# Three fast feed-forwards in two parts instead of five, with the seven-product pairs of a part in a row

## The reference

```python
D_FF = 2816
def _swiglu(x, w_in, w_out):
    a, b = jnp.split(x @ w_in, 2, axis=-1)
    return (jax.nn.silu(a) * b) @ w_out
...
    for l in range(DEPTH_2):
        mod = (jax.nn.silu(c) @ ada_w[l] + ada_b[l]).reshape(B, 3, 3, 1, D)
        n = _modulate(_rmsnorm_2(h, norm_g[l, 0]), mod[:, 0, 0], mod[:, 0, 1])
        h = h + 0.5 * mod[:, 0, 2] * _swiglu(n, ffn_w_in[l, 0], ffn_w_out[l, 0])
        ...
        n = _modulate(_rmsnorm_2(h, norm_g[l, 2]), mod[:, 2, 0], mod[:, 2, 1])
        h = h + 0.5 * mod[:, 2, 2] * _swiglu(n, ffn_w_in[l, 1], ffn_w_out[l, 1])
```

## Time and profile before

| what | value |
|---|---|
| median of 3 runs | 3290.63 us (3289.96 to 3294.26) |
| profiled execution, its own time | 3291.03 us |
| its span | 3289.2 us |
| PE busy | 3242.2 us (99%) |
| DVE busy | 2057.6 us (63%) |
| ACT busy | 1461.0 us (44%) |
| DMA | 435.21 MB, mean 132 GB/s |

### The profile page before, as it was taken

The page is one execution under the profiler, slowest core; times in us unless marked ns, Lnnn a source line. Parts: engine busy times, 40 slices in busy tenths (PEclk is TensorE's granted clock), DMA queues, the critical chain, the costliest instruction groups (busy, mean ns, idle before and its releaser), DMA issues.

```text
span 3289.2 us, 52037 instructions
## 1 busy us (share of the span) xinstructions
PE 3242.2 (99%) x22014; PEld 2741.7 (83%) x22014; DVE 2057.6 (63%) x3459; ACT 1461.0 (44%) x2496; POOL 213.5 (6%) x319
## 2 busy tenths in 40 slices
PE   8999999999999999999999999999999999999998
PEld 6878767888888888888778899989998877789997
DVE  6675764678666665665654665666565666466655
ACT  5233565335344422234553444454444455344443
POOL 1000000101000010100000011101010000001110
PEclk9999999999999999999999999999999999999999
DMA  4010102655544365643112366736675321227764
GB/s 152 27 61 31 39 27 96 219 193 185 184 147 147 110 242 192 240 158 108 57 46 88 99 190 174 199 110 174 188 176 158 113 81 47 82 84 178 192 177 120
DMA packets 121193, 435.21 MB, mean 132 GB/s; under 512 B 13936, under 2 KB 16048, under 8 KB 120320
## 3 DMA queue, kind: packets, MB, share of 16 engines
q1 hardware_dynamic: 80928, 286.30, 24.8%
q0 software_dynamic: 40032, 145.58, 17.7%
HBM read 401.41 MB, written 2.10 MB: 123 GB/s over the span
## 4 chain that ended last, share of the span: by engine, by line
PE 91%; DVE 5%; ACT 2%; DMA 1%; issue 0%; POOL 0%; DVEq 0%; ACTq 0%; POOLq 0%
PE ps_run L479 90%; PE ps_run L871 1%; DVE wl L2246 1%; ACT nrm L1369 1%; ACT wh L1369 1%; DMA st<-wst 0%; DVE nrm L2246 0%; DVE X L2253 0%; PE ps_run L1219 0%; DVE HL L2253 0%; DVE nrm L2253 0%; DVE msk L2250 0%; DMA st<-st 0%; ACT HH L1369 0%; ACT bias L1369 0%
## 5 line engine op out<-in xcount | busy, mean ns | idle before, releaser
L2246 DVE TENSOR_TENSOR wl<-st,wh 128x1024 fp32r<-128x1024 f32 (+1 forms) x592 | 721.2, 1219 | 596.2 <-ACT wh L1369 594.3
L479 PE MATMUL ps_run<-HH,wh 128*128 128x512 f32 (+1 forms) x2560 | 911.2, 356 | 11.3 <-DVE HL L2253 3.2
L479 PE MATMUL ps_run<-HH,wl 128*128 128x512 f32 (+1 forms) x2560 | 893.4, 349 | 0.0
L479 PE MATMUL ps_run<-HL,wh 128*128 128x512 f32 (+1 forms) x2560 | 891.3, 349 | 0.0
L1369 ACT ACTIVATE wh<-st 128x1024 fp32r<-128x1024 f32 (+1 forms) x592 | 619.8, 1049 | 586.6 <-PE ps_run L479 453.0
L479 PEld LDWEIGHTS ps_run<-HH,wh 128*128 128x128 f32 x2560 | 485.0, 189 | 82.9 <-DVE HL L2253 6.0
L479 PEld LDWEIGHTS ps_run<-HL,wh 128*128 128x128 f32 x2560 | 485.2, 190 | 63.2 <-issue 3.8
L479 PEld LDWEIGHTS ps_run<-HH,wl 128*128 128x128 f32 x2560 | 484.8, 189 | 63.0
L479 PE MATMUL ps_run<-AH,wh 128*128 128x512 f32 (+1 forms) x1152 | 444.5, 386 | 1.2 <-DVE AL L2246 1.2
L479 PE MATMUL ps_run<-AL,wh 128*128 128x512 f32 (+1 forms) x1152 | 438.3, 381 | 0.0
L479 PE MATMUL ps_run<-AH,wl 128*128 128x512 f32 (+1 forms) x1152 | 438.1, 380 | 0.0
(11 more groups left out here) (453 smaller groups left out, 4026.6 us busy)
## 6 DMA issues: line engine op xcount, KB each, us to landing
st<-wst SPq DMA_DIRECT2D x538, 512.0 KB, 3.4
mb<-ada POOLq DMA_DIRECT2D x144, 512.0 KB, 4.8
st<-wst POOLq DMA_DIRECT2D x54, 512.0 KB, 7.4
st<-st POOLq DMA_DIRECT2D x54, 512.0 KB, 4.6
cw<-cw POOLq DMA_DIRECT2D x4, 1024.0 KB, 6.3
X<-xT SPq DMA_DIRECT2D x8, 256.0 KB, 6.3
X<-xT POOLq DMA_DIRECT2D x8, 256.0 KB, 4.2
out<-X SPq DMA_DIRECT2D x16, 128.0 KB, 1.8
```

The source lines that it names most:

```text
L479: i = self.e.matmul(out, lhsT, rhs, start=start, stop=stop, skip_group_check=True)
L2246: self.e.tensor_tensor(out, a, b, op).then_inc(*self.w.done(*points))
```

## The change

The five parts become two, of the pairs 0 to 5 and 6 to 10, and the down products of a part stand behind its last pair, all eight outputs with 12 or 10 blocks each. Between two seven-product pairs of a part nothing is left. Since a pair's `tail` is now done during the next pair, DVE waits for its own last operation (`w.own()`) before it overwrites a tile that the pair before still reads. `PART_SLOTS` gives the first part 12 slots of `AH`/`AL` and the second 10, and ACT waits before it overwrites a slot of the first part until PE has finished that part's down products. The number of matmuls, of slabs and of adding transfers stays the same; DVE adds 16 down products to `X` in one feed-forward in place of 40.

```diff
-PARTS = ((0, 2), (2, 4), (4, 6), (6, 8), (8, 11))
-PART_SLOTS = ((0, 1, 2, 3), (4, 5, 6, 7), (0, 1, 2, 3), (4, 5, 6, 7), (0, 1, 2, 3, 8, 9))
+PARTS = ((0, 6), (6, 11))
+PART_SLOTS = (tuple(range(12)), tuple(range(10)))
...
-                if k == 4 and i == 7:
+                if k == 1 and i == 7:
                     self.last_linear((key, "down", k, i), specs, hi, lo, ready, outputs, after)
                 else:
-                    finish(self.linear((key, "down", k, i), specs, hi, lo, ready, outputs if k == 4 else beside))
+                    finish(self.linear((key, "down", k, i), specs, hi, lo, ready, outputs))
...
-                if k and p < a + 2:
-                    outputs_of(k - 1, range(4 * (p - a), 4 * (p - a) + 4))
             if k:
-                self.w.stamp("pe part", key, k - 1)
-        self.w.stamp("inputs free", after)
-        outputs_of(4, range(8))
+                self.w.stamp("inputs free", after)
+            outputs_of(k, range(8))
+            self.w.stamp("pe part", key, k)
         self.pad()
...
-        if k >= 2:
-            w.wait_ge("pe part", key, k - 2)
+        if k:
+            w.wait_ge("pe part", key, 0)
         self.half((key, "f", g), m.c1[0], m.AH[slots[0]])
...
-                if k and p < a + 2:
-                    for i in range(4):
-                        finish(self.spend(2 * (PARTS[k - 1][1] - PARTS[k - 1][0])))
-                        if i == 0:
-                            self.finish_pair()
-        self.finish_pair()
-        self.down(after, 4, 6)
+            self.finish_pair()
+            self.down(after, k, 2 * (b - a))
...
                 if step == 1:
+                    w.own()
                     summed(m.c1[x][:, part(0)], 0, x, name, "B", 1)
```

More of the change, by code:

```diff
@@ L2987, in fast_swiglu @@
                     self.plain_pair(key, p, slots, forms)
[L2988 to L2996, removed]
+            self.finish_pair()
+            self.down(key, after, k, into, iter(()), 2 * (b - a))
     def plain_pair(self, key, p, slots, forms):
```

## The result

The changed kernel takes 3421.32 us (median of 4 runs, 3420.60 to 3424.69) against 3291.08 for the kernel before beside it: a ratio of 1.0396 [1.0378, 1.0414], 130 us slower. The profiled execution has a span of 3419.6 us.

A forecast was written before the change was run, and what follows sets the result against it. The prediction took PE, busy 99%, as the bound, with a 17.3 us chain against 12.3 us allowed. Waits 136.5 plus clock 9 minus ends 4 made 141.5 us on 3291.0: 3432 us, range 3375 to 3500.

The forecast's parts named there:

- What bounds the kernel, and where the cover goes: PE, busy 99%, bounds the kernel; down products between pairs cover a transfer chain nearly as long as PE's work meanwhile.
- The turning point: Between two pairs, PE would just not wait if s2 landed within 12.3 us of the split of s4.
- T: In a repeated gap, the moment ACT starts on the late s2; the split of s4 was put at T + 10.0.
- The chain: From the split of s4 through slab 2's load, s1 and s2 to s2's landing: 5.0 + 7.75 + 4.53 = 17.3 us.
- the rival of fast adding transfers: In the gaps, s1 and s2 take a load's 3.4 us, chain 12.3, PE does not wait: 3286 us; chance 0.03.
- The gaps: 21 uncovered gaps between pairs: PE waits 5.0 us in a row's first, 7.1 in each repeated one, period 27.3.
- 3402 if the tail does not delay it: Sign of error: if the former pair's tail does not delay the split of s4, repeated gaps about 5.1 us, time about 3402.
- the term of 136.5 us for the waits: PE's waits in the gaps: 2 x 5.0 + 5 x 7.1 = 45.5 us per feed-forward, 136.5 for three.
- the 9 us for the clock: Half-clock work after waits, hidden between pairs, costs 1.5 us behind each of six last pairs of a row: 9 us.
- The ends: At the three feed-forward ends, ten blocks per output in place of 6 shorten PE's waits: 4 us gained, between 0 and 9.
- The sum: Whole kernel: 136.5 + 9 - 4 = 141.5 us on 3291.0 gives 3432.5, so 3432 us against the median.
- the bound of 34 us for the clock: Upper bound of the clock's cost, if the half-clock stretch lasts through all of step 2 behind the waits: 34 us.

## Why the prediction was right, point by point

**What bounds the kernel, and where the cover goes.** Right. The run without s1 and with s3 behind s2 shows it: the changed order with a chain of 10.9 us costs nothing, with 16.6 it costs 130 us. The turning point that the prediction gave, 12.3 us, holds for the first gap of a row: in all six of the changed kernel PE's wait was the chain less 12.3, to within 0.1 us (a chain of 17.0 and a wait of 4.7 in the first). It does not hold for the gaps behind it. There, by the prediction's own sum, the split of s4 ends at T + 10 and the pair is 20.2 us of work, so a chain longer than 10.2 makes the next pair later. The chain of 10.9 is all but free (4.2 us of waits in all) because a row has only three or four gaps and its first leaves 1.4 us to spare; the one of 10.8 costs as little (5.2), while 13.3 costs 48 us and 15.1 costs 94. So the rival of fast adding transfers had not only its premise wrong but also its condition: at 12.3 us each of the fifteen repeated gaps still costs 2.1, which gives about 3318 and not 3286.

**The chain.** 17.3 us predicted, 16.6 measured. Load and the issue of s1 are 5.3 (5.0 taken), s1 to the issue of s2 6.4 (7.75 taken), s2 to ACT's start 4.9 (4.53 taken). The sum is close by some luck, because s1, the one term that was too large, gained 1.3 us and the others gave back 0.7. The guess that s1 would stay as it was failed: its own mean over all 27 went from 6.7 us to 5.9. Why it became faster was not separated; in the changed kernel s3 doesn't slow it, as the run that moved s3 away shows.

**The gaps.** 21 waits were expected and 21 came. T to the split of s4 was 10.0 and measured 10.1; the period 27.3 and measured 26.8. The reason given for the 10.0, the tail, was half of it: with the tail away the clock holds the same moment, so the prediction's "3402 if the tail does not delay it" would have been wrong, as the run with the tail early showed (3419). With the clock restored the early tail brought 24 us (3412 to 3388).

**Waits and clock.** Here a size was off, in the term of 136.5 us for the waits and in the 9 us for the clock. The waits were 92.7 more, and 44.3 us went into slower work. The prediction let PE work 20.2 us in a repeated period at the full clock and wait 7.1; in truth it waited 4.6 of 26.8 (68.3 over 15) and worked for the rest, since slow work fills a wait that would have been there anyway. So the waits of 5 and 7 us that should have shown it came out as 4.2 and 4.6. That the clock hides between pairs was said and holds: with the clock restored only 8.9 us came back. Together, 145.5 predicted and 137.0 measured. Taken apart, the first gaps' waits (25 us) and what the fifteen repeated periods exceed 20.2 by (100) are 125 in place of 136.5, by the shorter chain; and behind the six last pairs of a row PE was busy for 26.7 us at half the clock, which lost 13.4 in place of 9. The two errors partly cancel. Why the run with extra matmuls brought back less than 13.4 was not separated; at 4.3 us they are longer than the shortest waits, 3.2 us.

**The ends.** 4 us predicted, 6.1 measured.

**The sum.** 141.5 predicted, 130.4 measured by the spans: 8.5 less from gaps and clock, 2.1 more gained at the ends, and 0.5 by which the terms and the spans differ. The upper end of the range was not what its terms give: with the bound of 34 us for the clock in place of 9, 3489 becomes 3514, and not 3500.

## What to carry to other kernels

Where an engine is busy for 99%, look for the chain that ends just before it wants its result, and compare that chain with the work that remains when something is taken out of between: here 16.6 against 12.3 us, in a chain that the list of waits before showed by 0.6 us in one place. Where such gaps follow each other, a late start also delays the next chain: here the turning point falls to 10.2 us. Such cover can be replaced by starting the chain earlier, but each queue on it has to be put in the order of need (SP's loads and POOL's sums both; the first alone gave 82 of 130 us, the second alone nothing, both 127). A clock that falls during waits costs little while a chain sets the pace, and to remove one of two things that hold the same moment shows nothing.

## What the runs showed of the hardware

**Of two adding transfers in flight, the later one pays.** With s3 issued 0.55 us ahead of s2 (without s1), s3 took 5.4 us and s2 7.4; with s2 ahead of s3 by 1.4 us on the mean, s2 took 5.3 and s3 6.9, at the same size of 512 KB, though s3 reads DRAM and s2 SBUF. In the two runs with s1 and s2 ahead of s3 by 0.57 us, s2 took 4.9 and 5.0, s3 7.3 and 7.6. The Trainium skill, DMA: Bandwidth & Descriptors, section Two DMAs through the same engine are not ordered, says that within one queue of a DMA engine descriptors start in order; that the transfer issued later was the slower one in either order, 7.4 and 6.9 us, fits this, but when single descriptors started was not read from a trace.

**What makes an adding transfer from DRAM slow is open.** In two runs no other sum was in flight during any s1, so only loads stood beside it. With s3 moved alone, s1 had 1.8 to 6.3 us of load time beside it (about one load at a time or less; one s1 at the head of a feed-forward had more) and took 5.1 to 6.6 us. With slab 2 first as well, fifteen of the 21 s1 in the gaps had 12.7 to 20.4 us of load time beside them and took 6.8 to 8.3 us, but the other six, with 8.9 to 10.6, took only 5.2 to 5.9. That is 1.8 to 2.5 loads at a time for the slow ones and 1.7 to 1.9 for the others, so the loads beside it alone don't tell which s1 is slow. This is read from all s1 of the two traces, not from a run that changed the loads alone.

**The half clock came back often and stayed for different times.** In the changed kernel each of PE's 21 waits of 3.2 to 7.6 us was followed by work at 0.50, in stretches of 3.4 to 10.2 us by the trace's clock records; in all they made PE's work some 44 us longer.
